# Branch C's prompt part: two dilated groups in one softmax over shared query tiles, and the join with tokens on partitions

## The reference, cut to what matters

```python
def dilated_group(q, k_all, v_all, q_idx, dil, n_keys, slopes):
    idx = q_idx[:, None] - dil * jnp.arange(n_keys)[None, :]
    ...
    s = jnp.einsum('bqhd,bqmhd->bhqm', q, kg) * (HEAD_DIM ** -0.5)
    s = s - slopes[:, None, None] * (dil * steps)
    lse = jax.nn.logsumexp(s, axis=-1)
    p = jnp.exp(s - lse[..., None])
    return jnp.einsum('bhqm,bqmhd->bqhd', p, vg), lse
...
    wts = jax.nn.softmax(jnp.stack(lses), axis=0)
    return jnp.sum(wts * jnp.stack(outs), axis=0)
```

## Time and profile before

| what | us |
|---|---|
| median of three runs | 2694.86 |
| the profiled execution | 2698.43 |
| its span | 2696.4 |
| block `c_prompt`, first instruction of it to first instruction of `c_sample` | 1152.97 to 1259.17 |
| of it, turning of values and keys | to 1161.4 |
| of it, 24 units | to 1231.4 |
| of it, the join | to 1258.9 |

### The profile page before, as it was taken

One profiled execution on the slowest core, in us unless ns is written; L12 is line 12 of the kernel. 1 busy time (PEld: TensorE's weight loads), 2 busy tenths in 40 slices (PEclk: granted clock), 3 DMA queues, 4 the chain that ended last, 5 costly groups with the idle time before them and its releaser, 6 DMA issues. The chain is left out here.

```text
span 2696.4 us, 45967 instructions
## 1 busy us (share of the span) xinstructions
PE 2301.4 (85%) x19363; PEld 2090.5 (78%) x19363; DVE 1226.7 (45%) x1835; ACT 421.7 (16%) x639; POOL 656.0 (24%) x598
## 2 busy tenths in 40 slices
PE   3995699769766776995599999798999999999995
PEld 3994688649434446974499999798999999999985
DVE  2336443221876671177123223118753762772652
ACT  4004212110751220032000001002100000110012
POOL 3110100001554331100012212143432432432331
PEclk6996899879888898997699999899999999999997
DMA  5140100041929985132511111211111111111112
GB/s 153 47 164 3 27 4 4 18 156 30 319 82 349 331 274 172 31 142 108 170 41 41 49 39 31 98 47 32 48 36 51 46 36 51 41 42 45 48 39 73
DMA packets 255424, 237.24 MB, mean 88 GB/s; under 512 B 22060, under 2 KB 243094, under 8 KB 253549
## 3 DMA queue, kind: packets, MB, share of 16 engines
q1 hardware_dynamic: 208096, 160.08, 19.3%
q10 hardware_dynamic: 39452, 53.37, 5.9%
q0 software_dynamic: 7680, 20.98, 2.3%
HBM read 211.10 MB, written 45.11 MB: 95 GB/s over the span
## 5 line engine op out<-in xcount | busy, mean ns | idle before, releaser
L134 PE MATMUL ps<-ml,fu_wh 128*128 128x352 f32 (+1 forms) x1248 | 410.4, 329 | 22.0 <-POOL fu_wl L128 16.9
L136 PE MATMUL ps<-mh,fu_wl 128*128 128x352 f32 (+1 forms) x1248 | 409.2, 328 | 0.0
L135 PE MATMUL ps<-mh,fu_wh 128*128 128x352 f32 (+1 forms) x1248 | 409.0, 328 | 0.0
L134 PEld LDWEIGHTS ps<-ml,fu_wh 128*128 128x128 f32 x1248 | 235.9, 189 | 23.9 <-POOL fu_wl L128 23.1
L128 POOL TENSOR_TENSOR fu_wl<-fu_wt,fu_wh 128x1024 fp32r<-128x1024 f32 (+2 forms) x84 | 191.4, 2279 | 246.0 <-DVE fu_wh L123 246.0
L135 PEld LDWEIGHTS ps<-mh,fu_wh 128*128 128x128 f32 x1248 | 236.7, 190 | 0.0
L136 PEld LDWEIGHTS ps<-mh,fu_wl 128*128 128x128 f32 x1248 | 235.5, 189 | 0.0
L134 PE MATMUL ps<-mx_l,wgh 128*128 128x352 f32 (+1 forms) x576 | 195.8, 340 | 22.3 <-POOL wgl L128 11.3
L136 PE MATMUL ps<-mx_h,wgl 128*128 128x352 f32 (+1 forms) x576 | 190.2, 330 | 0.0
L135 PE MATMUL ps<-mx_h,wgh 128*128 128x352 f32 (+1 forms) x576 | 190.1, 330 | 0.0
L134 PE MATMUL ps<-fu_al,fu_wh 128*128 128x384 f32 x528 | 176.6, 334 | 10.7 <-POOL fu_wl L128 7.1
(11 more groups left out here) (474 smaller groups left out, 4727.6 us busy)
## 6 DMA issues: line engine op xcount, KB each, us to landing
fu_wt<-in_w_up SPq DMA_DIRECT2D x44, 512.0 KB, 3.8
out_win_sample<-in_cache_win SPq DMA_DIRECT2D x8, 2040.0 KB, 38.1
bs_pk<-in_cache_sb_k SPq DMA_DIRECT2D x112, 128.0 KB, 7.7
bs_pv<-in_cache_sb_v SPq DMA_DIRECT2D x112, 128.0 KB, 7.7
wgt<-in_w_in SPq DMA_DIRECT2D x24, 512.0 KB, 4.1
bs_pk<-in_cache_sb_k POOLq DMA_DIRECT2D x80, 128.0 KB, 5.7
bs_pv<-in_cache_sb_v POOLq DMA_DIRECT2D x80, 128.0 KB, 5.9
fu_wt<-in_w_down SPq DMA_DIRECT2D x24, 384.0 KB, 3.2
```

Of the source, the lines that this page charges most:

```text
L134: nc.tensor.matmul(out, wh, xl, start=start, stop=False)
L135: nc.tensor.matmul(out, wh, xh, start=False, stop=False)
L136: return nc.tensor.matmul(out, wl, xh, start=False, stop=stop)
```

## The change

The units become 16. Eight joined units (J) come first: unit m takes the 128 queries with token number m modulo 8, for the second and the third group at once, against two key blocks of the second group (all keys with the same token number modulo 4) and one of the third, 384 scores per head and row, with one maximum and one sum. Eight units of the first group (F) follow, with 128 consecutive queries and up to 256 scores. All products have tokens on the output's partitions (`pT` as weights, the values as the moving operand, 64 columns), so the maximum and the sum stay columns of `res`: the ones and `dg` products go. ScalarE sums the exponentials along the row (`accum_out`).

A joined unit's rows are tokens m, m+8, ..., those of F consecutive ones. So each joined unit is written to DRAM (`scr_cj`) from GpSimd's queue, and when all eight have landed the whole is loaded back with consecutive tokens. `combine` joins the two in two halves of four tiles with small operations (8 columns) and three of 512 columns, TensorE turns the result (`final`), and ScalarE copies it to `g.oc`.

The turning of values, keys and new rows is no longer ahead of the units: it is twelve fills, one in each of the first twelve iterations (`fill` on TensorE, `filled` on ScalarE instead of VectorE). SP's stores wait for all twelve. The tables of values and keys and `pT` lie in the last two batches' places of `win1`, so only these two are loaded in `c_sample`; the first two batches of `win1` are loaded in `c_prompt`, after `win0` and ahead of the stores.

```diff
+        g.win1 = ctx.enter_context(nc.sbuf_tensor("cs_win1", [P, NB // 2, 13, 2 * P], F32))
...
+        fills = [("v", n, vts[n:n + 4]) for n in range(0, 24, 4)] + [("k", n, kts[n:n + 4]) for n in range(0, 13, 4)] + \
+                [("new", kv, [(gi, None) for gi in range(3)]) for kv in range(2)]
+        NF = len(fills)
+        units = [(J, m) for m in range(NT)] + [(F, m) for m in range(NT)]
...
-                eng.dma_start(bias[:, :, :, :], a["c_bias"]).then_inc(s["c"], 16)
+                eng.dma_start(jbias[:, :, :, :], a["c_jbias"]).then_inc(s["c"], 16)
+                eng.dma_start(bias[:, :, :], a["c_bias"]).then_inc(s["c"], 16)
                 load_windows(g, eng, g.win0, g.s_w, range(0, NB, 2))
+                load_windows(g, eng, g.win1, g.s_w, range(1, NB - 3, 2))
...
-                eng.wait_ge(s["te"], NTR)
-                eng.wait_ge(s["ne"], 2)
+                eng.wait_ge(s["te"], NF)
...
+            @block.gpsimd
+            def _(eng):
+                for m in range(NT):
+                    eng.wait_ge(s["oe"], m + 1)
...
+                    eng.dma_start(joined.rearrange("(i r) c -> r i c", r=8)[m], res[:, J, m, :]).then_inc(s["cj"], 16)
+                eng.wait_ge(s["cj"], 16 * NT)
+                eng.dma_start(res[:, J, :, :], joined.rearrange("(j p) c -> p j c", p=P)).then_inc(s["cl"], 16)
...
+                for i in range(NUN + 2):
+                    if i < NUN:
+                        scores(i)
+                    if i < NF:
+                        fill(i)
+                    if 1 <= i < NUN + 1:
+                        turn(i - 1)
+                    if i >= 2:
+                        weighted(i - 2)
+                    if i == NUN:
+                        final(0)
+                final(1)
```

More of the change, by code:

```diff
@@ L1985, in _, with scores @@
             @block.tensor
             def _(eng):
[L1987 to L1992, removed]
+                def scores(i):
+                    if i >= 2:
+                        eng.wait_ge(s["sc"], i - 1)
+                    kind, m = units[i]
+                    for x in parts(i):
+                        gi, kb = keys(i, x)
+                        for e in range(2):
+                            rows = slice(HD * e, HD * e + HD)
+                            q = qc[rows, gi, m * P:(m + 1) * P] if kind == F else qc[rows, gi, m:SEQ:8]
+                            mm = nc.tensor.matmul(g.ps[:, 2 * (i % 2) + e, x * P:(x + 1) * P], q,
+                                                  c_tile(qc[rows, 3 + gi, :], gi, kb), start=True, stop=True)
+                    mm.then_inc(s["s"], 1)
@@ L1999, in _ @@
-                eng.wait_ge(s["ne"], 2)
+                    what, n, tiles = fills[f]
+                    for q, (gi, m) in enumerate(tiles):
+                        if what == "new":
+                            mm = nc.tensor.transpose(g.ps[0:TS, 6 + f % 2, q * P:(q + 1) * P], qc[:, 3 + 3 * n + gi, SEQ:T], g.ident)
+                        else:
+                            mm = nc.tensor.transpose(g.ps[:, 6 + f % 2, q * P:(q + 1) * P],
+                                                     c_tile(qc[:, (6 if what == "v" else 3) + gi, :], gi, m), g.ident)
@@ new lines, in fill, with turn @@
+                    mm.then_inc(s["tr"], 1)
+                def turn(i):
+                    for e in range(2):
+                        eng.wait_ge(s["ex"], 2 * i + e + 1)
+                        if i:
+                            eng.wait_ge(s["pt"], 2 * (i - 1) + e + 1)
+                        for x in parts(i):
+                            mm = nc.tensor.transpose(g.ps[:, 4 + e, x * P:(x + 1) * P], sc[:, i % 2, e, x * P:(x + 1) * P], g.ident)
+                        mm.then_inc(s["t"], 1)
@@ L2000, in _, with final @@
+                def final(h):
+                    eng.wait_ge(s["fin"], h + 1)
+                    eng.wait_ge(s["sc"], NUN - 1)
+                    for q in range(4):
+                        mm = nc.tensor.transpose(g.ps[:, h, q * P:(q + 1) * P], res[:, F, 4 * h + q, values], g.ident)
+                    mm.then_inc(s["f"], 1)
                 for i in range(NUN + 2):
                     if i < NUN:
-                        gi, m = units[i]
-                        if i >= 2:
-                            eng.wait_ge(s["sc"], i - 1)
@@ L2005, in _ @@
[L2005 to L2011, removed]
```

261 lines of the change are left out of this document (147 added, 114 removed).

## The result

| | before | after |
|---|---|---|
| median, us (four runs each) | 2694.99 | 2663.70 |
| lowest and highest | 2694.41, 2698.82 | 2660.89, 2667.50 |
| the profiled execution, its span | 2698.43, 2696.4 | 2662.84, 2660.5 |
| block `c_prompt` in the trace | 106.2 | 77.9 |
| block `c_sample` in the trace | 52.85 | 50.0 |

The ratio is 0.9883 (95% interval 0.9868 to 0.9899): 31.3 us less, where 24.5 were forecast, and the time lies in the range.

What follows compares the result with a forecast made beforehand. Bound: the block of 106.2 us, by TensorE in the units, then VectorE's join chain. Fills through at 1205, stores 28.4 us, block end 1259.2 to 1234.7: 24.5 us less, 2694.9 to 2670; range 2658 to 2683.

Steps and rivals of the forecast that it cites:

- The stores end the block: SP's 74 stores wait for the last fill and take 28.4 us; block ends at 1234.7, engines at about 1225.
- Rival 3: SP's stores go out faster than before, so the engines' end at 1225 counts: 2660 us; chance 0.05.
- The start: VectorE's first operation waits for both biases until 1158, so TensorE can turn unit 0 from 1161.
- The fills: The fills inside the first twelve iterations are through on TensorE at 1204.2, ScalarE's last copy at 1205.
- the low clock: TensorE's early stretch of 7 us at the lower clock level, claimed to cost 2.6 us.
- The joined unit: TensorE's joined iteration: scores 1.75, fill 0.6, turns 0.95, products 1.6, together 4.9 us; other engines stay below.
- The lower bound: Joined iteration of 3.5 us if strides cost nothing (scores 0.98) and products ran at 0.08 a record.
- The engines' own end: Engines finish remaining units, join, turn and copy at about 1225, giving 10 us of cover before the stores' end.
- The round trip: Joined results through DRAM: store lands at 1207, load back at 1213 to 1230; join due at about 1216.
- rivals 2 and 4: Load back late: at 1230, 2677 us, chance 0.08; or very slow, landing at 1265, 2712 us, chance 0.03.
- Rival 1: Clock stays low through joined units, some 3 us in each of six iterations: 2686 to 2692 us; chance 0.09.
- The samples' block: Two window batches fewer to load there, but TensorE isn't waiting for them: nothing gained.

Runs made afterwards that it cites:

- e1: Changed kernel with SP's one wait for all twelve fills split into four gates: block 71.0 us against 77.9, total 2659.34 us.
- e3: Changed kernel with the joined results loaded back from DRAM four times in a row: block 81.1 us against 77.9, total 2663.64 us.
- e5: e1 with TensorE's turn back of the join's first half moved behind the last unit's products: block 69.9 us against 71.0, total 2657.09 us.
- e2: Changed kernel with contiguous columns for queries and keys in the joined units' scores: block 74.3 us against 77.9, total 2660.75 us.
- e4: Changed kernel with all twelve fills ahead of the units, copied by VectorE and ScalarE in turn: block 76.0 us against 77.9, total 2665.80 us.
- e8: e5 with halved bias load, packed query and key copies from the third joined unit, second window half loaded in `c_sample` again: block 66.1, total 2650.88 us.

## Why the prediction was right, and where its terms were off

**The stores end the block: right.** From the first store to the next block 29.9 us for 29.6 forecast, and e1 shows that they, and not the engines, were the end. Rival 3 (faster stores) fell: their pace is that of the earlier trace rows to 0.1 us.

**The start: right.** The turn of unit 0 was put at 8.0 us behind the block's start and came there (1160.26).

**The fills: 4.0 us earlier than forecast**, 48.0 us behind the start instead of 52.0. This is the term that was mis-sized, and it makes the block 3.8 us shorter than forecast. Some 1.8 us of it are the low clock, which was put at 2.6 and cost 0.8. The 2.6 us were taken from how contiguous scores stretch in the earlier trace rows, over 7 us; but here the low level ended 4 us behind the first turn, and the scores are strided and take 1.81 at 0.50 as at 1.00. What did stretch is little, the first turn by 0.5 us (1160.26 to 1161.73) and the next fill by 0.3 (1163.47 to 1164.27):

```profile
1160.26 1.54 PE L2062 MATMUL ps<-cf,cq_sc 128*128 128x128 f32 x6 [2.29 <-ACT cq_sc L2136]
1161.73 1.81 PE L2038 MATMUL ps<-qc 64*128 64x128 f32 x12
1163.47 0.96 PE L2052 MATMUL ps<-cf,qc 128*128 128x128 f32 x4
1164.27 0.82 PE L2062 MATMUL ps<-cf,cq_sc 128*128 128x128 f32 x6
```

Part of that is luck: with the same instructions there, this iteration took 5.4 to 5.5 us in the traces of e1, e3 and e5, where the clock came back later, and 4.9 here. The rest of the 4.0 us is the joined iteration, 4.61 to 4.69 instead of 4.9 (fill and products were each put a wait too high), some 1.5 us in six of them, and 0.7 us in the iterations and the copy behind.

**The joined unit: right in its parts.** 1.74 for 1.75, 0.49 for 0.6, 0.93 for 0.95, 1.45 for 1.6. The lower bound's first condition (strides cost nothing) isn't the case, as e2 shows; its 0.98 for such scores was no bound, as 0.86 was measured. Nor do the products run at its 0.08 a record: they are 0.12 apart. VectorE needs 2.4 us in an iteration and ScalarE 3.2, so TensorE stays the bound, with fills on ScalarE.

**The engines' own end: the number by luck**, 71.2 us behind the start for 72 forecast. From the last fill's copy it took 23.3 us (1200.21 to 1223.49) instead of 20, and the earlier fills hid that. The sum left out a wait: TensorE stands 2.0 us for the join's first half, and turns that half back, before the last unit's products, and these took 1.81 us instead of 1.1, with the clock at 0.56 from 1215.0 to 1217.6.

```profile
1215.07 0.92 PE L2083 MATMUL ps<-cf,cq_res 128*128 128x128 f32 x4 [2.03 <-DVE cq_res L2177]
```

e5 takes 1.1 us of it back. The cover came out as 6.7 instead of 10, as the stores started 4 us earlier and the engines ended 0.8 earlier.

**The round trip: both bounds too high.** The lower one was 5.7 us for a store and 5.7 for the load; they were 2.4 and 4.9. The rows used were transfers among many others, and here the DMA engines had little else to do (their share is 0.07 from 1190 to 1199). The error lay on the harmless side, and rivals 2 and 4 fell with it; by e3's pace it would have taken two loads more for the join to wait.

**Rival 1 fell, but not its mechanism.** The clock was back at 1.00 from 1164 on. The Trainium skill, "TensorE: Matmul & The Clock Gate", Part 4: PE-mode transpose, whose rule on turns spoke for it, isn't borne out for joined units, in which 24 of 34 records are matrix products. In e4 the granted clock was 1.00 while TensorE did nothing but turns (1161 to 1168), and 0.50 behind them. The low clock is what the rule would lead one to expect, the 1.00 is not; and 3 us of nothing lie between, which no run here parts from the turns. The price was too high as well: 1.8 us in e4's iterations, which have no fill, not 3, again because strided scores don't stretch.

**The samples' block, "nothing gained": in the trace 2.85 us less, which belongs to the clock and not to the change.** TensorE there, 16 turns and the products behind them, before and after:

```profile
1272.07 3.67 PE L2194 MATMUL ps<-cf,cs_win 128*128 128x128 f32 x16 [0.76 <-ACT cs_kT L2248]
...
1301.16 8.43 PE L2232 MATMUL ps<-cs_win,cs_qm 128*32 128x128 f32 x208
```
```profile
1243.07 1.97 PE L2268 MATMUL ps<-cf,cs_win 128*128 128x128 f32 x16 [0.76 <-ACT cs_kT L2322]
...
1270.46 7.27 PE L2306 MATMUL ps<-cs_win,cs_qm 128*32 128x128 f32 x208
```

The clock in these two stretches of turns, before and after:

```profile
1272.00:1276.00 4.00, 3.94 (x28) 3.61 (x32) 0.73 (x2) 0.50 (x2) 0.00 (x0) 0.53 1.02 408
```
```profile
1243.00:1245.00 2.00, 1.93 (x20) 1.76 (x21) 0.74 (x2) 0.51 (x2) 0.00 (x0) 1.00 0.00 0
```

1.7 us in these turns and 1.2 in the products (granted clock 0.69 before, 0.80 after) make up the 2.85. It isn't the six window transfers that moved away: e4 has them moved and these turns took 3.67 us (the block 53.0), e8 has them back and they took 1.97 (50.9). In eleven kernels with the same work for the engines in this block it took 49.5 to 53.0. So of the 35.9 us between the two spans 28.3 are the block's, 2.85 this, 0.7 an earlier start, and about 4 lie in the merge and the stages behind it. Their code is the same in all eleven kernels, and in the eleven traces they take 1377.8 to 1384.4 us (1384.4 before, 1380.3 after), so 4 us there are scatter. Of the 6.8 us by which the medians beat the forecast (31.3 for 24.5), 3.8 are the block's, then; the other 3 lie outside it, where the engines' work is the same before and after, and are luck.

**What is not shown.** The stores, the fills and the round trip were each changed by themselves (e1, e4, e3). The joined units and the new join were not undone alone; what they give rests on their rows.

## What to carry to other kernels

When work is moved off the critical path, ask for each wait of the DMA queues which event now opens it: here a change that shortened the engines' work by 35 us gave 28, since stores that had 60 us of slack hung on the last of twelve fills, and splitting that one wait gave back the other 7. Price a stretch of low clock by how the very operations in it stretch, not by those of another form. And look at idle engines at the front of a block before adding work to a busy one: the same copies cost 2.6 us on VectorE and nothing on ScalarE.

## What of the hardware was not expected

- The stride's price falls on TensorE's moving operand above all: for 12 records with 128 columns each, at the full clock, 0.69 us for strided keys and 0.19 for strided queries, beside 0.86 for the plain ones; and strided scores take the same 1.81 us at both levels of the clock.
- The granted clock was 1.00 in a stretch of turns alone and in 3 us of nothing behind it, then fell, and stayed at 0.50 for at least 14 us of nearly full work (e4, 1171 to 1185).
- Two strided copies of 128x1024 took 5.9 us on VectorE and 5.0 on GpSimd side by side, and 4.1 on ScalarE beside GpSimd, whose own two took 4.1 there. So GpSimd's were 0.8 us slower while VectorE copied; whether VectorE's 5.9 come from the stride or from GpSimd's company no run here tells.
